# Seven block products per eight in the last projection of a two-layer kernel, with GpSimd's sums as left operands

## The reference

```python
b_g, c_g, v = jnp.split(h @ w_in, 3, axis=-1)
z = causal_conv3(c_g * v, conv_w)
out = (b_g * z) @ w_out                        # the last projection: 4096 x 1024 x 1024
x = x + (1 + g1)[:, None, :] * out
hn = modulate(rmsnorm(x, norm2_g[i]), sh2, sc2)
g_prob = softmax(hn @ wg + bg); e_logits = hn @ we + be     # router: 4 groups, 32 experts
gi = top_1(g_prob); ev, ei = top_2(e_logits within group gi)
```

## Time and profile before

| | |
|---|---|
| median of 3 runs (lowest to highest) | 6161.75 us (6160.59 to 6164.22) |
| profiled execution | 6154.4 us |
| its span from first to last instruction | 6152.6 us |
| mean granted clock of TensorE, share of full | 0.976 |
| busy shares | TensorE 95%, VectorE 62%, ScalarE 35%, GpSimd 34% |

### The profile page before, as it was taken

The page is one execution under the profiler, slowest core; times in us unless marked ns, Lnnn a source line. Parts: engine busy times, 40 slices in busy tenths (PEclk is TensorE's granted clock), DMA queues, the critical chain, the costliest instruction groups (busy, mean ns, idle before and its releaser), DMA issues. The chain is left out here.

```text
span 6152.6 us, 83067 instructions
## 1 busy us (share of the span) xinstructions
PE 5849.7 (95%) x28274; PEld 4775.9 (78%) x28275; DVE 3795.6 (62%) x5360; ACT 2133.1 (35%) x3188; POOL 2086.2 (34%) x1978
## 2 busy tenths in 40 slices
PE   7999989999899999999989999998997999999994
PEld 5876668888678888888868788887775888888884
DVE  6889945554455555555536688876776554556555
ACT  2334432222144334444335323321113333444434
POOL 6555538870122222222324533101112222223222
PEclk9999999999899999999999999999998999999997
DMA  4564664432267666767647756644445656777767
GB/s 153 175 193 150 189 230 148 140 135 83 84 220 214 204 174 209 217 201 212 188 132 269 268 184 202 198 156 162 152 155 191 194 163 188 212 214 244 212 199 282
DMA packets 621295, 1152.42 MB, mean 187 GB/s; under 512 B 122708, under 2 KB 219572, under 8 KB 620089
## 3 DMA queue, kind: packets, MB, share of 16 engines
q1 hardware_dynamic: 422256, 799.04, 38.0%
q0 software_dynamic: 94176, 315.82, 18.8%
q10 hardware_dynamic: 104682, 35.19, 2.2%
HBM read 863.32 MB, written 286.29 MB: 187 GB/s over the span
## 5 line engine op out<-in xcount | busy, mean ns | idle before, releaser
L2288 DVE SCALAR_TENSOR_TENSOR m_o<-m_pO,m_weight_of,m_gate 128x512 f32<-128x512 f32 x316 | 233.6, 746 | 714.1 <-POOLq L1933 377.4
L2255 DVE TENSOR_TENSOR m_w_lo<-m_w_raw,m_w_hi 128x1024 fp32r<-128x1024 f32 x512 | 596.1, 1214 | 0.1
L1915 POOL COPY m_gather_now<-m_gather_of 128x1 int32 (+1 forms) x161 | 182.5, 1133 | 1147.0 <-DMA x<-m_o,m_scatter_now 913.7
L2086 ACT ACTIVATE m_xT_hi<-m_pX 128x512 fp32r<-128x512 f32 x320 | 191.4, 599 | 1000.3 <-PE m_pB L146 994.3
L144 PE MATMUL m_pA<-m_w_lo,m_xT_hi 128*128 128x512 f32 x1280 | 517.4, 404 | 14.2 <-DVE m_xT_lo L2266 14.2
L2074 ACT ACTIVATE m_w_hi<-m_w_raw 128x1024 fp32r<-128x1024 f32 x512 | 505.6, 1053 | 50.3 <-DMA m_w_raw<-in_moe_w_dram 29.2
L2027 PE MATMUL m_pO<-m_w_lo,m_hT_hi 128*128 128x512 f32 x1280 | 514.1, 402 | 0.4 <-ACT m_hT_hi L2091 0.2
L146 PE MATMUL m_pA<-m_w_hi,m_xT_hi 128*128 128x512 f32 x1280 | 503.0, 393 | 0.0
L145 PE MATMUL m_pA<-m_w_hi,m_xT_lo 128*128 128x512 f32 x1280 | 500.4, 391 | 0.0
L2027 PE MATMUL m_pO<-m_w_hi,m_hT_hi 128*128 128x512 f32 x1280 | 499.9, 391 | 0.0
L144 PE MATMUL m_pB<-m_w_lo,m_xT_hi 128*128 128x512 f32 x1280 | 498.3, 389 | 0.0
(11 more groups left out here) (531 smaller groups left out, 13591.2 us busy)
## 6 DMA issues: line engine op xcount, KB each, us to landing
m_w_raw<-in_moe_w_dram SPq DMA_DIRECT2D x384, 1024.0 KB, 7.4
conv_op_raw<-xr SPq DMA_DIRECT2D x84, 1024.0 KB, 5.4
glu_ada<-in_ada_w_dram POOLq DMA_DIRECT2D x96, 256.0 KB, 3.2
a_x<-in_x_dram SPq DMA_DIRECT2D x32, 512.0 KB, 3.4
a_ada<-in_ada_w_dram POOLq DMA_DIRECT2D x64, 256.0 KB, 3.4
s_u<-u SPq DMA_DIRECT2D x64, 256.0 KB, 2.7
s_r<-k SPq DMA_DIRECT2D x64, 256.0 KB
glu_x<-in_x_dram SPq DMA_DIRECT2D x32, 512.0 KB, 5.0
```

What stands on the lines that cost most here:

```text
L1915: pool.tensor_copy(gx[:], gidx[:, bass.ds(t, 1)]).then_inc(gi_ready, 1)
L2086: act.activation(xT_hi[:, 4 * q:4 * q + 4, :], pX[:, 4 * q:4 * q + 4, :], ACT.Copy).then_inc(xt_hi, 1)
L2255: tt(W13[s][1][:, m, k:k + 2, :], W13[s][0][:, m, k:k + 2, :], W13[s][2][:, m, k:k + 2, :].bitcast(F32), ALU.subtract).then_inc(w13_lo, 1)
L2288: dve.scalar_tensor_tensor(out=ob[:, n, :], in0=pO[:, n, :], scalar=wslot[:, bass.ds(tile_, 1)], in1=gate2[:, n, :], op0=ALU.mult, op1=ALU ...
```

## The change

- `project` keeps only its `glu` form. A new phase `project_out` does the last projection over 16 pairs of tiles (even and odd) with the scheme of seven: 7 operations per pair, each of 4 blocks x 3 = 12 products of 128x512 in one bank of four. VectorE adds the banks into the rows of x directly, in seven slots per pair, one behind each operation; bank 0 is copied out by ScalarE (`keep`).
- The seven left operands (128x512 each) are three halves of the source rows as they are, and four sums of them, made by GpSimd (`left_sums`, 1 to 4) from SBUF to SBUF. The high half of each is made by ScalarE, the low half by VectorE, six operations ahead.
- The gate (1 + g1) goes into the weights: GpSimd multiplies it in `conv_in` into `conv_w_out` and makes the four sums of weight blocks, in 16 chains (`turn`), four behind the stores of each of groups 7 to 10, into the DRAM tensor `wt`. A chain waits for the stores of the one before. SP loads weight blocks 0 and 1 when all are stored, at the sixth operation from the end, and the operand of the last operation behind them; then the odd source rows, blocks 2 and 3, the even rows. Blocks 0 to 2 and two left operands are split in `conv_in`, block 3 is loaded there, 4 to 6 in `project_out`.
- The sum of squares moves from VectorE to ScalarE (`square`).
- The end of the phase on VectorE is written out anew.

The sums, and the chains in `conv_in` with SP's and (last) ScalarE's side; `NEXT_W` is {OPS - 5: 0, OPS - 3: 1, OPS - 2: 2}:

```diff
+            def left_sums(p, which):
+                o, e = odd[p % 2], even
...
+                    tt(sum1[:], flat(e[:, 0:KH, :]), flat(e[:, KH:, :]), ALU.add).then_inc(sums, 1)
...
+                    tt(sum2[:], sum1[:], flat(o[:, 0:KH, :]), ALU.subtract).then_inc(sums, 1)
...
+                    tt(raw[3][:], o[:, 0:KH, :], e[:, 0:KH, :], ALU.subtract).then_inc(sums, 1)
...
+                    tt(flat(raw[6][:]), flat(o[:, KH:, :]), sum2[:], ALU.subtract).then_inc(sums, 1)
...
+            def turn(i):
+                kk, q = seven.turns[i]
+                (a, b_), tt = pieces, pool.tensor_tensor
+                for h in range(2):
+                    if i:
+                        pool.wait_ge(turn_st[h], 16 * i)
...
+                for h in range(2):
+                    pool.dma_start(a[:, 2 * h:2 * h + 2, :], next_view[kk][q][h]).then_inc(turn_ld, 16)
+                pool.dma_start(gate_piece[:], gate_view[q].broadcast_to([P, 2, P])).then_inc(turn_ld, 16)
+                pool.wait_ge(turn_ld, 48 * i + 48)
+                d = Chain(pool, turn_step, 6 * i)
+                d(pool.tensor_scalar(gate_piece[:], gate_piece[:], 1.0, None, ALU.add))
+                wide = a[:].rearrange("p (h n) f -> p h n f", h=2)
+                d(tt(wide, wide, gate_piece[:].unsqueeze(1).broadcast_to([P, 2, 2, P]), ALU.mult))
...
+                pool.dma_start(to(0), a[:]).then_inc(turn_st[0], 16)
+                d(tt(b_[:, 3, :], a[:, 3, :], a[:, 1, :], ALU.subtract))
...
+                pool.dma_start(to(4), b_[:]).then_inc(turn_st[1], 16)
...
+                for i in range(4 * (g - 7), 4 * (g - 6)) if 7 <= g < 11 else ():
+                    turn(i)
+                    if i % 4 == 1:
+                        store(g, 2)
...
                 if n == OPS - 6:
-                    for k in range(6):
-                        sp.dma_start(n_raw[:, k, :], next_view[k]).then_inc(n_w_ld[k], 16)
...
+                    for q in range(2):
+                        sp.wait_ge(turn_st[q], 16 * len(seven.turns))
+                    next_weights(0)
+                    next_weights(1)
...
+                if n in NEXT_W:
                     act.wait_ge(prod, 3 * n)
+                    act.wait_ge(n_w_ld[NEXT_W[n]], 16)
+                    act.activation(ahead.w_hi[NEXT_W[n]][:], ahead.w_raw[NEXT_W[n]][:], ACT.Copy).then_inc(n_w_hi, 1)
+                if n == OPS - 4:
+                    act.wait_ge(src_ld[0], 16)
```

More of the change, by code:

```diff
@@ L1316, in project @@
         block = ctx.enter_context(nc.Block())
-        order = (2, 3, 0, 1) if glu else (0, 1)
+        order = (2, 3, 0, 1)
         KQ = NB_
@@ L1535, in _ @@
             chosen(dve.tensor_scalar(routes.base[:], io32[:], float(T), None, ALU.mult))
-            if glu:
-                low(0, 0)
-            else:
-                dve.sem_inc(tlo[0], 1)
-            for q in range(KD if glu else 0):
+            low(0, 0)
+            for q in range(KD):
                 dve.wait_ge(w_hi_ready, q + 1)
@@ L1609, in out_h @@
                 act.activation(hT[:], pH[:], ACT.Copy).then_inc(ht_out, 1)
-            if glu:
-                act.sem_inc(var, 1)
-            if glu:
-                high(0, 0)
-            else:
-                act.sem_inc(thi[0], 2)
-            for q in range(KD if glu else 0):
+            act.sem_inc(var, 1)
+            high(0, 0)
+            for q in range(KD):
                 act.wait_ge(w_ld[q], 16)
@@ L1627, in body @@
                         high(*at(i, s, 1))
-                    if glu:
-                        gate(i, s)
-                    elif not first:
-                        out_lT(*at(i, s, -2))
+                    gate(i, s)
                     if not (first and s == 0):
@@ L1654, in products @@
                 pe.wait_ge(tlo[s], i + 2)
-                if not glu:
-                    pe.wait_ge(out_read, n + 1)
-                elif not (isinstance(n, int) and n == 0):
+                if n != 0:
                     pe.wait_ge(gated, 2 * n)
-                first, second = ((1, 0), (2, 0)) if glu else ((0, KD // 2), (1, 0))
                 def rest():
@@ L2433, in __init__ @@
         assert not sums and not mixes
+        self.turns = [(kk, q) for kk in range(KH) for q in range(4)]
         self.small = [(c, kk, j) for c in range(2, CHUNKS) for kk in range(KH) for j in range(3)]
@@ L2867, in _ @@
                         store(g, 1)
+                for i in range(4 * (g - 7), 4 * (g - 6)) if 7 <= g < 11 else ():
+                    turn(i)
+                    if i % 4 == 1:
+                        store(g, 2)
+                if g not in range(7, 11) and g + 1 < OPS // SEVEN:
+                    store(g, 2)
                 if g + 1 < OPS // SEVEN:
-                    store(g, 2)
                     store(g, 3)
@@ L3004, in _ @@
                         summed(n, i, r - 2, kept[r - 1][JS[i]])
-                        if ahead and i == 0:
+                        if follows and i == 0:
                             op_low(n + 2, 1)
```

695 lines of the change are left out of this document (563 added, 132 removed).

## The result

The changed kernel takes 6285.19 us, median of 4 runs (6276.51 to 6291.75), against 6161.27 beside it: a ratio of 1.0199, 95% interval 1.0182 to 1.0217. It is slower by 124 us; I had forecast 75 slower, with 6275 as the upper end.

The account below looks back on a forecast made before the run. TensorE was taken to bound the last projection before the change. From the profiled 6154.4 us, +54 for the stage and +20 for the hand-over gave 6228, and the runs' median offset of 7.35 made 6236; range 6190 to 6275.

Parts of the forecast that it names:

- The step that failed: GpSimd's weight chains in the stage before: 13.4 us each, four fit a 57 us group, TensorE undisturbed until the end.
- my +20: Hand-over before the last projection: the last four chains delay weight blocks and operands, 20 us more; bounds +8 and +30.
- the 4.4 at the start: Stage start: VectorE's late halves and constants, 4.4 us before, no longer stand ahead of operation 0; counted in the stage's +54.
- the walk: Predicted timeline, chance 0.60: last four chains from 4116.5 to 4170.7, and two pairs of the stage in 62.5 us.
- The step that decides: Stage: eight records ahead of GpSimd's fourth sum hold ScalarE and TensorE, six times; two pairs take 62.5 us, against 53.2.
- Rivals 1 and 2: Stage: records hold nobody, only VectorE's batch pair felt, 6160 us, 0.08; or TensorE stays the bound, 6138 us, 0.08.
- rival 3: Hand-over: the chains are done in time, at 10 us each, and it costs 0; 6216 us, chance 0.14.
- The clock: Stage: after each of six TensorE waits the lower granted clock loses some 2 us, 12 us in all, bounds 0 and 18.
- The stage's sum: Last projection: 75 + 375 + 12 + 23.5 + 31 = 516.5 us; 520 with store and exchange, against 466, so +54.
- VectorE beside GpSimd: Stage: each GpSimd sum slows VectorE by 0.2 us, at most 0.9; bounds 0 and 3.6 us a pair.
- Rival 4: Stage: GpSimd and VectorE exclude each other nearly always, 3.6 us more on each of 16 pairs; 6266 us, chance 0.10.
- The gain: Stage on TensorE: seven operations make a pair 23.9 us instead of 26.6; over sixteen pairs 43 us less.

Follow-up runs that it names:

- e2: Changed kernel with the sixteen weight chains spread 4, 3, 3, 3, 3 over five groups instead of four each over four: 6241.1 us, ratio 1.0136.
- e5: Changed kernel with chains alternating between two buffer sets, the next chain's loads issued in the middle of a chain: 6234.0 us, ratio 1.0117.
- e1: Changed kernel with the eight records of a batch behind GpSimd's fourth sum instead of ahead of it: 6219.8 us, ratio 1.0101.
- e8: e6 with GpSimd's first and second sums of every pair but the first cut from 512 to 8 columns: 6162.9 us, ratio 1.0001.
- e13: e11 with the parts of choose spread over both pairs, ranks and place later, records around the fourth sum: 6156.0 us, ratio 0.9995.
- e7: e6 with the odd tile's transposes, router halves and router sum one operation later on TensorE: 6194.7 us, ratio 1.0050.
- e9: e6 with a PSUM bank of their own for the ranks of a batch: 6171.4 us, ratio 1.0019.
- e14: e13 with VectorE reading the even tile's logits ahead of three additions: 6161.2 us, ratio 1.0003.
- e11: e9 with choose cut into three parts inside the pair, and ranks, place and records moved into the next pair: 6178.2 us, ratio 1.0028.
- e12: e11 with choose left in one piece, only ranks, place and records moved into the next pair: 6173.1 us, ratio 1.0018.
- e6: Changed kernel with the edits of both e5 and e1: 6170.9 us, ratio 1.0014.
- e4: Changed kernel with a chain's loads waiting only for the first of the previous chain's two stores: 6266.0 us, ratio 1.0172.

## Why the prediction was wrong, point by point

**The step that failed: "Four in a group of 57 us fit, so TensorE isn't disturbed until the end."** The way to the stage grew by 48.5 us where my +20, less the 4.4 at the start, makes 15.6. That is 33 of the 49 us that were missing, and with the 4.4 the hand-over's 52.9 in place of 20 are outside my bound of 30. By my own figures four chains of 13.4 and four stores of 0.7 took 56.4 of the 57 us, a margin of half a us, and I didn't ask what happens beyond it: an overrun isn't lost once, it adds up over the groups. The first twelve chains took 16.85 us each with their stores, and the last four therefore started 34.3 us later than walked. From there on the walk held: the last four took 13.9 us each for 13.4, and from SyncE's going on (4208.56) to the first product of the stage it was 44.3 us, where the walk has 44.7. The parts that I had short: the gate is a third load that lands last (2.12 us of issues and 3.45 of landing for my 4.3), the second store's own issue of 0.8, and the operations while VectorE works (the gate 0.84 to 1.64, the product up to 2.10). The four sums, 0.46 each where nothing disturbs them, I had too long at 0.84. The z stores that are late in the same queue I didn't have at all. e2 and e5 show the cause from two sides, with fewer chains to a group and with shorter ones.

**The step that decides: right, each size a little high.** Eight records ahead of the fourth sum, ScalarE idle 13.9 us (some 14 forecast), the halves 9.45 us late (10 to 12 forecast), a cycle of 64.85 us for 62.5 and 2 of clock. e1 takes it away: 54.69, where I expected about 53. Rivals 1 and 2 are out, and rival 3 (chains done in time) with them.

**The clock: right in kind.** After each wait the products start at the lower level. The six cycles carry it, 0.4 us more each than forecast.

**The stage's sum** came to 58.9 us from first to last product for the forecast 51.5 (485.5 less 434.0). Five of the 7 us lie outside the six cycles: 6 x 64.85 = 389.1 leave 103.8 for pairs 0 to 2 and 15 instead of 98.5, and pair 0 alone has waits of 1.2, 1.8 and 5.0 us at its banks. Behind the last product I had 31 us up to the last place, and it took 32.0 for 24.1 before.

**VectorE beside GpSimd: the term was too small, and hidden.** 0.2 us for a sum was 0.52 to 0.55, inside my bound of 0.9. In the changed kernel it hardly showed, since VectorE stood idle behind the records anyway; with the records out of the way 64 sums are some 34 us of VectorE's time. I wrote that the earlier trace rows bear out that both engines are slowed, not that one stands still. The rows of this kernel show that one does stand still. A subtraction of 16 columns, 0.17 us before, takes 1.24 in six of seven batches, and it ends with GpSimd's third sum; a bank read that starts with a sum keeps its 0.68:

```profile
4411.32 1.28 POOL L1842 TENSOR_TENSOR ahead_left_raw<-ahead_src,ahead_src 128x512 f32<-128x512 f32 x1 [9.08 <-PE cout_p L145]
...
4411.40 1.24 DVE L1896 TENSOR_TENSOR cout_tmp<-cout_logits,cout_m 128x16 f32<-128x16 f32 x1
...
4527.72 0.68 DVE L1963 TENSOR_TENSOR cout_x_odd<-cout_p,cout_x_odd 128x512 f32<-128x512 f32 x1
4527.74 1.29 POOL L1847 TENSOR_TENSOR ahead_left_raw<-ahead_src,ahead_sum 128x512 f32<-128x512 f32 x1 [9.29 <-PE cout_p L145]
```

In the cycle shown above, too, the subtraction at 4505.02 ends 0.55 us after the sum does (4505.55), the normalisation at 4506.21 takes 2.10 for 1.28 behind the sum that ends at 4507.23, and that sum, begun while the subtraction ran, takes 1.52 for 1.27. The Trainium skill's rule (SBUF — State Buffer, "Who interferes with whom"), by which a VectorE instruction with two SBUF inputs and a GpSimd one that reads SBUF exclude each other for the whole instruction, agrees with these rows. What was too high is the step from it to 1.3 us for every sum: the average is 0.52 to 0.55 because many sums fall beside bank reads, which have one input in PSUM, beside idle time, or beside the end of an instruction. Rival 4 had the right mechanism; its price of 0.9 a sum lies above VectorE's 0.52 to 0.55 and at the upper end of the stage's 0.73 to 0.87.

**The gain: there, and given back at both ends.** TensorE's busy time in the stage fell from 427.1 to 384.7 us in e8 at nearly the full clock, about the 43 us that I had reckoned (e8 leaves sums out, which TensorE doesn't feel; with all of them it is 389.1 in e13). The same change raises VectorE's from 301 to 357 us and more, so that what the seven products save becomes a shorter stage only with VectorE's work evenly spread: in e13 the stage is 19.4 us shorter than before. It is spent outside of it: 9.6 us on the way, and 10.3 behind the last product. That last part is in every version: with the routes of the kernel before, 1527.0 to 1531.3 us follow the last product, and 1518.5 did before. I had 7 of those us in the forecast and no experiment touched them. What of the 9.6 us is the weight blocks' loading and what the chains is open too; it wasn't tried alone.

## What to carry to other kernels

Work that is put into a periodic gap has to fit with its stores, its neighbours and a margin: an overrun of 10 us in a period came out as 34 us after three periods, and it reached everyone in the same queue. Where an instruction joins a queue, ask who waits for the entry behind it; eight DMA issues that hurt nobody became the critical path as soon as one sum stood behind them. And when a wait is taken away, look first whether the engine that ended it is late as a whole: of the runs from e7 on that keep all the work, only e13, which moved 5 us of it into the other pair, gained; e7, e9 and e14 changed order or banks, e11 and e12 moved 2 us, and the stage got no shorter. Last, set the stage's own time beside that of the kernel before, and then what lies ahead of it and behind it: here the stage of e6 was already shorter, and the whole loss stood at the two ends.

## What the runs showed of the hardware that I had not expected

- A VectorE instruction with two SBUF inputs stands still until GpSimd's running sum ends: 16 columns took 1.24 us for 0.17, 512 columns 1.08 for 0.68, while bank reads beside a sum kept 0.68. Averaged over the stage a sum of 128x512 costs VectorE 0.52 to 0.55 us, from 34 to 96 sums. GpSimd's own sum mostly takes 1.27 to 1.30 us, and 1.52 where it begins inside such a subtraction.
- Loads issued while a store of the same queue was still on its way landed after 5.5 us at the median instead of 4.1 (e4), and of 41 us of hidden waits 13 were gained.
- The idle time alone doesn't tell what clock the transposes behind it get. Eight of them take 1.06 us at the full clock and 1.94 at the lower level. Behind 2.28 us of idle time it was 1.06 (e13), behind 3.96 1.06 to 1.09 (changed kernel), behind 5.21 1.89 to 1.94 (e11); but behind 3.43 once 1.06 and twice 1.5 (e14), and behind 4.43 1.94 three times and 1.09 to 1.26 three times, in turn (e9, two of them below).

```profile
4429.79 1.94 PE L2188 MATMUL cout_pH<-ident,cout_hn 128*128 128x128 f32 x8 [4.43 <-DVE cout_logits L1892]
...
4484.73 1.19 PE L2188 MATMUL cout_pH<-ident,cout_hn 128*128 128x128 f32 x8 [4.43 <-DVE cout_logits L1892]
```
